# A two-layer transformer block on one core: context gates moved ahead of the keys' squares, level items computed in strips of 32, low-rank operands loaded and split first

## The chip, the core and the metric

The kernel runs on one NeuronCore of a Trainium2 chip. The metric is the time of one execution on the device, in microseconds. An execution of the kernel before took 905.5 us as the median of three runs (902.12 to 905.83). A fourth execution was profiled and took 903.21 us; its trace spans 901.3 us.

Engines are named as in the profile: PE is TensorE's matmul, PEld its weight load, DVE is VectorE, ACT is ScalarE, POOL is GpSimd, SP is SyncE.

## What is computed

A hybrid layer (attention beside gated linear attention, GLA) and a second layer (mLSTM and a gated embedding), both with a squared-ReLU MLP, over 256 tokens of width 1024 with a context of 256 tokens. The change touches GLA alone. What it computes, cut from the reference:

```python
def gla_log_decay(lowrank, w_gk, b_gk):
    g = jax.nn.log_sigmoid((lowrank @ w_gk + b_gk).astype(jnp.float32)) / GLA_GATE_NORM
    return gla_heads(g, GLA_DK)
...
    def step(state, inp):
        qc, kc, vc, gc = inp
        b = jnp.cumsum(gc, axis=2)
        o_inter = jnp.einsum('bhid,bhde->bhie', qc * jnp.exp(b), state)
        diff = jnp.where(mask, b[:, :, :, None, :] - b[:, :, None, :, :], -jnp.inf)
        a = jnp.einsum('bhid,bhjd,bhijd->bhij', qc, kc, jnp.exp(diff))
        o = o_inter + jnp.einsum('bhij,bhje->bhie', a, vc)
...
def gla_final_state(k, v, g):
    b = jnp.cumsum(g, axis=2)
    return jnp.einsum('bhtd,bhte->bhde', k * jnp.exp(b[:, :, -1:] - b), v)
```

It runs forward and backward in time, for 4 heads of 128 key dimensions, over the 256 tokens, with the context's final state (`gla_final_state`) as the first state.

## The kernel before

**Products.** Every large matrix product is computed in three terms: each operand is split into a rounded high part (ScalarE, `hi_part`, L1323) and the rest (VectorE, `lo_part`, L1788), and TensorE adds hi x hi, lo x hi and hi x lo (`product`, L751). Weights come from one stream of 512 KB units through a ring of four buffers (`raw`); SP issues a unit when the unit four places back has been split. A tile of weights is four units. `w_hi` and `w_lo` hold two tiles, so that a tile is split while the one before it is used; ScalarE may begin a tile when TensorE is through with the tile two places back.

**Order.** The order of all work is one list of steps, `PLAN1` for the first mixer. Each engine walks the list and does its share of each step, and semaphores tie the shares together. `woven` writes the steps of one tile: 8 or 16 pieces of six matmuls with the splits (`round`, `cut`) of the next tile and a list of side steps spread evenly between them. The tiles in question, in order, are gk and gq, lr (the low-rank product), kv, gv0, gv1, aq0, aq1, ga0, and later wbg0.

**The low-rank operands.** POOL loads nine small tensors (L710 to L715), all of which count up one semaphore. At the step `prepare` ScalarE waits for all nine and rounds `gate_w`, the signs and then `lr_w` and `mg_w`; VectorE subtracts. TensorE's `lr` group (L811, L813) waits for the low part of `lr_w`.

**Level items.** The triangular scores of a head are built by levels: the diagonal, then one item per width 128, 64, 32, ..., 1, where the decay between a query and a key is taken in two factors around a boundary of that width. There are 9 items a head and 36 in all (`N_ITEMS`). Each walks through the engines in three steps of `gla_level(s)`: VectorE forms the arguments (L2169), ScalarE their exponentials (L1530, two instructions), VectorE multiplies with keys and queries (`gx_z`, L2176), TensorE multiplies two 128x128 blocks (L1021; the diagonal item L1014) into one of three banks, and VectorE puts the wanted entries into the score tile `gx_s` (L2149 diagonal, L2153 width 128, L2157 masked for all others; `lv_put` counts). A put always reads 128x256. `level_steps` lists the 39 values of s with the decays, gates and query products of each head between them, 57 steps; they are spread over kv, gv0, gv1 and aq0.

**The context's state.** In tile aq1 the steps `gstate` 0 to 5 run a chain over the heads: gate matmuls (L984), three ScalarE passes for log(1 + exp) (L1489 to L1491), VectorE's L2113, cumulative sums on TensorE (L972, L974), their exponential (L1504), VectorE's product with the keys (L2108), and the state (L960). The gate matmuls of head 0 wait for all puts. The steps just before, `rope k 0` and `rope k 1`, sum the squares of the attention keys on VectorE (L2012, L2013), and in the second of them ScalarE waits for the variance (L1836) to begin its inverse root.

**The turn.** `yturn` (L897) transposes a quarter of the merged branches; the first of four is a side step of wbg0.

## Time and profile before

| | before |
|---|---|
| median of three runs | 905.5 us (902.12 to 905.83) |
| profiled execution | 903.21 us, span 901.3 us |
| TensorE matmul busy | 876.1 us, 97% |
| VectorE busy | 627.0 us, 70% |
| ScalarE busy | 482.6 us, 54% |
| mean granted clock of TensorE | 0.996 |
| moved by DMA | 162.25 MB, mean 180 GB/s |

How to read it: an engine's busy time is the union of its instructions' times, and matmuls overlap by their pipeline, so a busy PE is not yet PE at its pace; the distance from one start to the next tells the pace. The profile is of one execution, so sums of its durations are compared with its own 903.21 us. The granted clock is 1.00 at 2.4 GHz and 0.50 at 1.2 GHz.

### The profile page before, as it was taken

To read this page: it belongs to the slowest core of one execution; us is meant where nothing else is said; L and a number is where in the kernel's file an instruction comes from. 1 tells how busy PE (TensorE), PEld (TensorE's weight loads), DVE (VectorE), ACT (ScalarE), POOL (GpSimd) and SP (SyncE) were. 2 spreads that over 40 slices of the span, in tenths; PEclk is the share of its full clock that TensorE was granted. 3 is DMA by queue.
4 is the path that set the end of the run, shared out by engine and by line. 5 is a ranking of instruction groups with operands and counts; after the bars stand their busy time and mean duration, and the time that the engine had idled before them with its cause. 6 is when DMAs were issued, how large, how long until landed. Compare 5 with 4: busy or idle time off the path is not lost.

```text
span 901.3 us, 14166 instructions
## 1 busy us (share of the span) xinstructions
PE 876.1 (97%) x5136; PEld 755.5 (84%) x5136; DVE 627.0 (70%) x997; ACT 482.6 (54%) x758; POOL 13.1 (1%) x26
## 2 busy tenths in 40 slices
PE   5999999899999999999999999999999999999996
PEld 3878888787788888889999998998888999999985
DVE  3579979779788988865555557767787855555575
ACT  4576555465666565565444444454655644444454
POOL 0110000000000000000000000000000000000001
PEclk9999999999999999999999999999999999999999
DMA  9954323226347777735555558254444765555531
GB/s 364 374 141 140 117 71 112 99 94 204 124 142 234 260 266 257 242 126 189 187 187 186 186 186 280 94 187 138 145 138 142 248 223 205 180 190 191 183 119 48
DMA packets 45296, 162.25 MB, mean 180 GB/s; under 512 B 5500, under 2 KB 5644, under 8 KB 45248
## 3 DMA queue, kind: packets, MB, share of 16 engines
q1 hardware_dynamic: 43200, 156.78, 51.6%
q0 software_dynamic: 1328, 4.16, 1.6%
q8 instruction: 32, 0.52, 0.3%
q10 hardware_dynamic: 720, 0.65, 0.2%
q14 instruction: 16, 0.13, 0.0%
HBM read 160.52 MB, written 1.05 MB: 179 GB/s over the span
## 4 chain that ended last, share of the span: by engine, by line
PE 77%; DVE 11%; ACT 4%; DMA 3%; issue 3%; POOL 1%; POOLq 0%; DVEq 0%; SPq 0%; ACTq 0%
PE bank L751 65%; DVE w_lo L1788 3%; PE bank L939 1%; PE bank L1021 1%; ACT w_hi L1323 1%; DMA raw<-in_stream 1%; DMA arena<-in_early 1%; DVE small L1818 1%; PE bank L929 1%; PE bank L1221 1%; DMA gate_row<-in_b_gates 1%; PE bank L1041 1%; PE bank L1036 1%; DVE act_lo L1788 1%; PE bank L946 1%
## 5 line engine op out<-in xcount | busy, mean ns | idle before, releaser
L1788 DVE TENSOR_TENSOR w_lo<-raw,w_hi 128x1024 fp32r<-128x1024 f32 x244 | 288.3, 1220 | 150.7 <-ACT w_hi L1323 150.0
L1323 ACT ACTIVATE w_hi<-raw 128x1024 fp32r<-128x1024 f32 x244 | 245.8, 1050 | 193.2 <-PE bank L751 163.0
L751 PE MATMUL bank<-w_hi,act_lo 128*128 128x512 f32 (+1 forms) x728 | 293.2, 403 | 0.3 <-DVE w_lo L1788 0.2
L751 PE MATMUL bank<-w_lo,act_hi 128*128 128x512 f32 (+1 forms) x728 | 282.8, 388 | 0.0
L751 PE MATMUL bank<-w_hi,act_hi 128*128 128x512 f32 (+1 forms) x728 | 282.2, 388 | 0.0
L751 PE MATMUL bank<-act_lo,w_hi 128*128 128x256 f32 x640 | 182.9, 286 | 1.4 <-DVE act_lo L1788 0.9
L751 PE MATMUL bank<-act_hi,w_hi 128*128 128x256 f32 x640 | 181.0, 283 | 0.0
L751 PE MATMUL bank<-act_hi,w_lo 128*128 128x256 f32 x640 | 181.0, 283 | 0.0
L751 PEld LDWEIGHTS bank<-w_lo,act_hi 128*128 128x128 f32 x728 | 136.7, 188 | 29.3
L751 PEld LDWEIGHTS bank<-w_hi,act_lo 128*128 128x128 f32 x728 | 137.2, 188 | 27.4 <-issue 1.4
L751 PEld LDWEIGHTS bank<-w_hi,act_hi 128*128 128x128 f32 x728 | 137.3, 189 | 25.4 <-issue 1.0
L751 PEld LDWEIGHTS bank<-act_lo,w_hi 128*128 128x128 f32 x640 | 122.6, 192 | 4.9 <-DVE act_lo L1788 2.8
L751 PEld LDWEIGHTS bank<-act_hi,w_hi 128*128 128x128 f32 x640 | 122.7, 192 | 0.5
L751 PEld LDWEIGHTS bank<-act_hi,w_lo 128*128 128x128 f32 x640 | 122.7, 192 | 0.0
L1788 DVE TENSOR_TENSOR act_lo<-arena,act_hi 128x512 fp32r<-128x512 f32 x64 | 41.7, 686 | 5.3 <-ACT act_hi L1323 4.6
L1818 DVE SCALAR_TENSOR_TENSOR small<-raw,silu_c,small 128x512 f32<-128x512 f32 x56 | 42.0, 750 | 4.9 <-DMA raw<-in_stream 3.0
L1530 ACT ACTIVATE arena<-arena 128x256 f32<-128x256 f32 x64 | 24.1, 426 | 24.1 <-DVE arena L2169 23.9
L1323 ACT ACTIVATE act_hi<-arena 128x512 fp32r<-128x512 f32 (+1 forms) x33 | 20.0, 630 | 31.3 <-DVE arena L1915 25.5
L1394 ACT ACTIVATE arena<-bank 128x512 f32<-128x512 f32 x42 | 24.7, 590 | 14.2 <-PE bank L751 14.0
L2176 DVE TENSOR_TENSOR arena<-arena 128x512 f32<-128x512 f32 x32 | 21.9, 685 | 4.9 <-ACT arena L1530 4.8
L1021 PEld LDWEIGHTS bank<-arena 128*128 128x128 f32 x128 | 18.8, 190 | 5.1 <-issue 1.9
L939 PEld LDWEIGHTS bank<-arena 128*128 128x128 f32 x128 | 16.7, 191 | 7.2 <-issue 5.7
(264 smaller groups left out, 753.7 us busy)
## 6 DMA issues: line engine op xcount, KB each, us to landing
raw<-in_stream SPq DMA_DIRECT2D x278, 512.0 KB, 4.4
arena<-in_early SPq DMA_DIRECT2D x16, 512.0 KB, 10.7
res<-in_x SPq DMA_DIRECT2D x2, 512.0 KB, 4.2
arena<-in_ctx SPq DMA_DIRECT2D x2, 512.0 KB, 11.3
res<-in_x POOLq DMA_DIRECT2D x1, 1024.0 KB, 10.6
arena<-in_norm_final POOLq DMA_DIRECT2D x1, 512.0 KB, 4.3
arena<-in_ple_b POOLq DMA_DIRECT2D x1, 512.0 KB, 5.2
out<-arena ACTq DMA_DIRECT2D x2, 256.0 KB, 2.7
```

The lines of the kernel that those rows point to most:

```text
L751: last = pe.matmul(o, left, right, start=start and m == 0, stop=stop and m == 2, skip_group_check=shared)
L929: pe.matmul(psum[4 + i % 2][:, :], q_t[:, h, t * P:(t + 1) * P], k_t[:, h // (QH // KVH), :], start=True, stop=True).then_inc(score_done, 1)
L939: last = pe.matmul(psum[7][:, t * P:(t + 1) * P], kv[:, c, c0:c0 + HD], prob_t[:, c, :], start=(c == 0), stop=(c == 3))
L946: last = pe.transpose(psum[6][:, c * P:(c + 1) * P], prob[:, j % 3, c * P:(c + 1) * P], ident)
L1021: last = pe.matmul(o[:, t * P:t * P + P], z[:, 0, tile[t]], z[:, 1, queries], start=True, stop=True)
L1036: pe.matmul(o, gx_s[h][:, SCORE_BLOCK[j, t], :], gv[:, j, h * DV:(h + 1) * DV], start=(j == 0), stop=False)
L1323: return act.activation(o, i, ACT.Copy)
L1394: act.activation(o, i, ACT.Copy, scale=scale).then_inc(evac_act, 1)
L1530: ins = act.activation(gx_z[k % 3][:, m].rearrange("p (n h t) -> p n h t", h=2, t=LEVELS[k % N_LVL]), crossed(gx_d[k % 2], m, LEVELS[k % N ...
L1788: return dve.tensor_tensor(o, x, hi.bitcast(F32), ALU.subtract)
L1818: ins = dve.scalar_tensor_tensor(out=ada_sum, in0=w, scalar=c, in1=ada_sum, op0=ALU.mult, op1=ALU.add)
L2176: dve.tensor_tensor(gx_z[k % 3], gx_z[k % 3], keys_queries(h), ALU.mult).then_inc(lv_z, 1)
```

## The change

Four things are changed.

1. The gate matmuls, the three ScalarE passes of context head 0 leave `gstate` 0 and become a step `gsfirst` in tile aq0, ahead of `rope k 0`. VectorE's share stays in `gstate` 0.
2. Level items other than width 128 are computed by strips. A 128-token block is cut into four groups of 32 keys; each is its own matmul with 32 output partitions, and only with the 32 queries that it needs (64 at width 64). The diagonal and the widths 16 to 1 are gathered in a small tile `gx_c` of 128x2x32 by VectorE, with masks and puts of 32 columns. The items of width 128, 64 and 32 (`COPIED`) are copied into `gx_s` by ScalarE, without masks, in one, two and four instructions. A new step `expand` lets ScalarE copy `gx_c` into the diagonal blocks of `gx_s`, four instructions a head; `gla_out` waits for it (`gx_full`), and VectorE's diagonal item of head h waits for that of head h - 2. The list of level steps has 61 entries.
3. POOL issues the loads of `small`, `wgk` and `signs` first, on their own semaphore. `prepare` moves up by one piece and waits for these three alone, ScalarE rounds `lr_w` and `mg_w` ahead of `gate_w` and the signs, and VectorE converts a mask of 160 columns instead of 896. The side steps after `prepare` are shifted.
4. `yturn 0` comes behind the eighth piece of wbg0 instead of the seventh.

The core of the diff:

```diff
+COPIED = (1, 2, 3)
+PUT_AT, _n = {}, {True: 0, False: 0}
+for _i in range(N_ITEMS):
+    _k = _i % PER_HEAD in COPIED
+    _n[_k] += 1
+    PUT_AT[_i] = (_k, _n[_k])
...
             out.append(("queries", h - 1))
+            out.append(("expand", h - 1))
...
-    sides = [[], [("prepare",)], cut("kv", 0), [("evac", "gk", 2)] + cut("kv", 1), [("evac", "lr", 0), ("lrcut",)],
-             cut("kv", 2), cut("kv", 3), [("gate", 0)], [("evac", "gk", 3), ("log_decay", 0)]]
+    sides = [[("prepare",)], cut("kv", 0), cut("kv", 1), [("evac", "gk", 2)],
+             [("evac", "lr", 0), ("round", "kv", 2), ("lrcut",), ("cut", "kv", 2)], cut("kv", 3), [], [("gate", 0)],
+             [("evac", "gk", 3), ("log_decay", 0)]]
...
-    p.woven("aq0", lv[c:] + [k[0], k[1]])
+    p.woven("aq0", lv[c:] + [("gsfirst",), k[0], k[1]])
...
-    p.woven("wbg0", [None] * 6 + [y[0]] + [None])
+    p.woven("wbg0", [None] * 7 + [y[0]])
...
+            for target, name in ((small[:, 0:384], "small"), (wgk, "wgk"), (signs, "signs")):
+                pool.dma_start(target, a[name]).then_inc(small_in, 16)
             pool.dma_start(consts[:, 1:6], a["consts"][:, 1:6]).then_inc(params_in, 16)
-            for target, name in ((small[:, 0:384], "small"), (wgk, "wgk"), (rope[:, :, :, :], "rope"),
-                                 (mask_in, "lvl_mask"), (signs, "signs")):
+            for target, name in ((rope[:, :, :, :], "rope"), (mask_in, "lvl_mask")):
...
-            pool.dma_start(p_in, a["p_t"]).then_inc(p_loaded, 16)
+            pool.dma_start(p_in, a["p_t"]).then_inc(small_in, 16)
...
-                if h < GH:
-                    if h == 0:
-                        pe.wait_ge(lv_put, N_ITEMS)
-                        pe.wait_ge(gx_g, GH)
-                    else:
-                        pe.wait_ge(gs_g, h)
...
+                if 0 < h < GH:
+                    pe.wait_ge(gs_g, h)
+                    gla_context_gate(h)
+
...
+                if h == 0:
+                    pe.wait_ge(lv_put, PUT_AT[N_ITEMS - 1][1])
+                    pe.wait_ge(lv_copied, len(COPIED) * GH)
+                    pe.wait_ge(gx_g, GH)
...
                 if n >= 3:
-                    pe.wait_ge(lv_put, n - 2)
+                    wait_put(pe, n - 3)
                 o = level_bank(n)
                 tile = [slice(0, P), slice(P, T)]
                 if e == 0:
-                    for t in range(2):
-                        last = pe.matmul(o[:, tile[t]], gk_x[:, h, tile[t]], gq_x[:, h, tile[t]], start=True, stop=True)
+                    keys, queries = gk_x[:, h], gq_x[:, h]
                 else:
                     k = h * N_LVL + e - 1
                     pe.wait_ge(lv_z, k + 1)
-                    z = gx_z[k % 3]
+                    keys, queries = gx_z[k % 3][:, 0], gx_z[k % 3][:, 1]
+                if e == 1:
                     for t in range(2):
-                        queries = tile[1 - t] if e == 1 else tile[t]
-                        last = pe.matmul(o[:, t * P:t * P + P], z[:, 0, tile[t]], z[:, 1, queries],
-                                         start=True, stop=True)
+                        last = pe.matmul(o[:, tile[t]], keys[:, tile[t]], queries[:, tile[1 - t]], start=True, stop=True)
+                else:
+                    n_cols = 64 if e == 2 else 32
+                    for t in range(2):
+                        for p in range(4):
+                            first = t * P + (64 * (1 - p // 2) if e == 2 else 32 * (p ^ 1) if e == 3 else 32 * p)
+                            last = pe.matmul(o[32 * p:32 * p + 32, t * n_cols:(t + 1) * n_cols],
+                                             keys[:, t * P + 32 * p:t * P + 32 * p + 32], queries[:, first:first + n_cols],
+                                             start=True, stop=True, skip_group_check=True)
...
+                pe.wait_ge(gx_full, h + 1)
...
-                if h < GH:
-                    act.wait_ge(gs_mm, h + 1)
-                    log1p_exp(gs_a.rearrange("p t d n -> p (t d n)"), psum[4][:, :], gs_ln, h)
+                if 0 < h < GH:
+                    gla_context_gate(h)
...
+            def gla_copy(n):
+
+                h, e = n // PER_HEAD, n % PER_HEAD
+                act.wait_ge(lv_mm, n + 1)
+                bank, to = level_bank(n), gx_s[h]
+                blocks = lambda rows_, w: bank[rows_, 0:2 * w].rearrange("p (b i) -> p b i", b=2)
+                if e == 1:
+                    ins = act.activation(to[:, 2:4, :], blocks(slice(0, P), P), ACT.Copy)
+                elif e == 2:
+                    for a_, b_ in ((0, 64), (64, 0)):
+                        rows_ = slice(a_, a_ + 64)
+                        ins = act.activation(to[rows_, 0:2, b_:b_ + 64], blocks(rows_, 64), ACT.Copy)
+                else:
+                    for p in range(4):
+                        rows_, c0 = slice(32 * p, 32 * p + 32), 32 * (p ^ 1)
+                        ins = act.activation(to[rows_, 0:2, c0:c0 + 32], blocks(rows_, 32), ACT.Copy)
+                ins.then_inc(lv_copied, 1)
+
             def gla_level(s):
+                n = s - 3
+                if 0 <= n < N_ITEMS and PUT_AT[n][0]:
+                    gla_copy(n)
...
+            def gla_expand(h):
+
+                wait_put(act, (h + 1) * PER_HEAD - 1)
+                for p in range(4):
+                    rows_ = slice(32 * p, 32 * p + 32)
+                    ins = act.activation(gx_s[h][rows_, 0:2, rows_], gx_c[rows_, h % 2], ACT.Copy)
+                ins.then_inc(gx_full, 1)
...
-                    act.wait_ge(params_in, 16 * N_PARAMS)
+                    act.wait_ge(small_in, 16 * N_SMALL)
+                    hi_part(lr_w[:, :, 0:32], small[:, 0:256].rearrange("p (k n) -> p k n", k=KC)).then_inc(small_hi_done, 1)
+                    hi_part(mg_w[:, :, 0:16], small[:, 256:384].rearrange("p (k n) -> p k n", k=KC)).then_inc(small_hi_done, 1)
                     hi_part(gate_w, wgk).then_inc(small_hi_done, 1)
                     hi_part(gate_x[6 * RANK:GATE_K], signs).then_inc(small_hi_done, 1)
-                    hi_part(lr_w[:, :, 0:32], small[:, 0:256].rearrange("p (k n) -> p k n", k=KC)).then_inc(small_hi_done, 1)
-                    hi_part(mg_w[:, :, 0:16], small[:, 256:384].rearrange("p (k n) -> p k n", k=KC)).then_inc(small_hi_done, 1)
...
-                if 0 <= n < N_ITEMS:
+                if 0 <= n < N_ITEMS and not PUT_AT[n][0]:
...
-                    to = gx_s[h]
...
-                        dve.scalar_tensor_tensor(out=to[:, 0:2, :], in0=blocks, scalar=2.0,
-                                                 in1=ident.unsqueeze(1).broadcast_to([P, 2, P]), op0=ALU.mult,
-                                                 op1=ALU.mult).then_inc(lv_put, 1)
-                    elif e == 1:
-                        dve.tensor_copy(to[:, 2:4, :], blocks).then_inc(lv_put, 1)
+                        if h >= 2:
+                            dve.wait_ge(gx_full, h - 1)
+                        ins = dve.scalar_tensor_tensor(out=c, in0=blocks(whole, 32), scalar=2.0,
+                                                       in1=diag_block[:, :].unsqueeze(1).broadcast_to([P, 2, 32]), op0=ALU.mult,
+                                                       op1=ALU.mult)
                     else:
-                        dve.wait_ge(lv_put, n)
-                        mask = lvl_mask[:, e - 2, :].unsqueeze(1).broadcast_to([P, 2, P])
-                        dve.copy_predicated(to[:, 0:2, :], mask, blocks).then_inc(lv_put, 1)
+                        dve.wait_ge(lv_put, PUT_AT[n][1] - 1)
+                        mask = lvl_mask[:, e - 4, :].unsqueeze(1).broadcast_to([P, 2, 32])
+                        ins = dve.copy_predicated(c, mask, blocks(whole, 32))
+                    ins.then_inc(lv_put, 1)
...
+                    dve.wait_ge(small_hi_done, SMALL_HI["gate_w"])
...
                     dve.wait_ge(params_in, 16 * N_PARAMS)
+                    dve.tensor_reduce(diag_block[:, :], ident.rearrange("p (b i) -> p i b", b=4), AX, ALU.add)
                     dve.tensor_copy(lvl_mask[:, :, :], mask_in).then_inc(masks_ready, 1)
...
-    masks = np.zeros((P, N_LVL - 1, P), np.float32)
-    for n, s in enumerate(LEVELS[1:]):
-        same = i // (2 * s) == j // (2 * s)
-        masks[:, n] = same & ((i % (2 * s) < s) != (j % (2 * s) < s))
+    row, col = np.arange(P)[:, None] % 32, np.arange(32)[None, :]
+    masks = np.zeros((P, N_LVL - 3, 32), np.float32)
+    for n, w in enumerate(LEVELS[3:]):
+        same = row // (2 * w) == col // (2 * w)
+        masks[:, n] = same & ((row % (2 * w) < w) != (col % (2 * w) < w))
```

## Rows read from the trace of the kernel before

**Rows 1.** The page, part 1: busy us (share of the span) xinstructions.

```profile
PE 876.1 (97%) x5136; PEld 755.5 (84%) x5136; DVE 627.0 (70%) x997; ACT 482.6 (54%) x758; POOL 13.1 (1%) x26
```

**Rows 2.** Stretches: us, busy us (count) by engine, PE clock, DMA share, GB/s.

```profile
70.00:158.00 88.00, 86.60 (x452) 72.64 (x451) 80.15 (x137) 50.95 (x104) 0.00 (x0) 1.00 0.33 107
...
124.00:143.00 19.00, 18.20 (x93) 14.66 (x91) 17.09 (x29) 10.62 (x22) 0.00 (x0) 1.00 0.37 113
...
171.30:174.70 3.40, 3.40 (x15) 3.40 (x16) 3.14 (x10) 0.60 (x2) 0.00 (x0) 0.50 0.00 0
```

**Rows 3.** Timeline, 168 us: start, us, engine, line, form, count [idle before <-releaser].

```profile
167.79 0.39 PE L751 MATMUL bank<-w_lo,act_hi 128*128 128x512 f32 x1
...
171.27 0.80 PE L972 MATMUL bank<-arena,consts 128*128 128x128 f32 x2 [3.09 <-DVE arena L2113]
...
166.80 0.21 ACT L1424 ACTIVATE stat<-stat 128x8 f32<-128x8 f32 x1 [7.74 <-DVE stat L1836]
...
166.59 0.17 DVE L1836 TENSOR_SCALAR stat<-stat 128x8 f32<-128x8 f32 x1
...
170.52 0.69 DVE L2113 SCALAR_TENSOR_TENSOR arena<-bank,arena 128x512 f32<-128x512 f32 x1 [3.75 <-ACT arena L1491]
```

**Rows 4.** Timeline at 176 us, VectorE and TensorE.

```profile
175.31 0.69 DVE L2108 TENSOR_TENSOR arena<-arena 128x512 f32<-128x512 f32 x1
...
177.31 1.89 PE L960 MATMUL bank<-arena 128*128 128x256 f32 x8
```

**Rows 5.** TensorE's waits, 50 to 235 us: total us, times, longest.

```profile
PE bank L1021 <- DVE arena L2176: 1.4, 3, 0.6
```

**Rows 6.** Timeline at 56 us, TensorE and ScalarE.

```profile
56.05 0.39 PE L751 MATMUL bank<-w_lo,act_hi 128*128 128x512 f32 x1
57.15 0.42 PE L811 MATMUL bank<-act_hi,small_hi 128*64 128x512 f32 x1 [0.71 <-DVE small_lo L1788]
...
53.99 1.71 ACT L1323 ACTIVATE gate_r<-arena 98x1024 fp32r<-98x1024 f32 x2 [0.96 <-DMA gate_row<-in_b_gates]
```

**Rows 7.** Timeline at 77 us, VectorE.

```profile
77.26 0.41 DVE L2153 COPY res<-bank 128x256 f32<-128x256 f32 x1
77.59 0.68 DVE L2169 TENSOR_TENSOR arena<-arena 128x512 f32<-128x512 f32 x1
```

**Rows 8.** Timeline at 126 us, VectorE's z and TensorE's item.

```profile
125.75 0.69 DVE L2176 TENSOR_TENSOR arena<-arena 128x512 f32<-128x512 f32 x1 [4.59 <-ACT arena L1530]
...
126.60 0.67 PE L1021 MATMUL bank<-arena 128*128 128x128 f32 x4
```

**Rows 9.** Groups by form, ScalarE: count | busy us, mean ns | idle.

```profile
L1346 ACT ACTIVATE arena<-arena 128x256 f32<-128x256 f32 x2 | 0.8, 408 | 0.5 <-DVE arena L1982 0.5
...
L1425 ACT ACTIVATE stat<-stat 128x2 f32<-128x2 f32 x9 | 1.8, 204 | 0.3
```

**Rows 10.** Timeline at 79 us, TensorE around one level item.

```profile
78.66 0.39 PE L751 MATMUL bank<-w_lo,act_hi 128*128 128x512 f32 x1
...
79.57 0.40 PE L751 MATMUL bank<-w_hi,act_hi 128*128 128x512 f32 x1
```

**Rows 11.** Timeline at 18 us, TensorE around one modulation strip (L1243).

```profile
17.86 0.28 PE L751 MATMUL bank<-act_hi,w_lo 128*128 128x256 f32 x1
18.07 0.64 PE L1243 MATMUL bank<-arena,small 128*32 128x256 f32 x8
...
18.86 0.28 PE L751 MATMUL bank<-act_hi,w_hi 128*128 128x256 f32 x1
```

**Rows 12.** Chain of work that ended last: start, us, line, count.

```profile
278.67 0.86 PE bank L1041 x4
```

**Rows 13.** Timeline at 57 us, weight loads of TensorE.

```profile
57.12 0.13 PEld L811 LDWEIGHTS bank<-act_hi,small_hi 128*64 128x64 f32 x1 [1.11 <-issue]
57.18 0.11 PEld L813 LDWEIGHTS bank<-act_lo,small_hi 128*32 128x32 f32 x1
```

**Rows 14.** Table of stretches, as in rows 2.

```profile
230.00:390.00 160.00, 159.97 (x790) 131.57 (x789) 130.83 (x214) 96.16 (x154) 4.02 (x8) 1.00 0.65 215
```

More of the change, by code:

```diff
@@ L380 @@
 UP0 = {"a": 0, "b": 2 * FF_STEPS}
-N_FIRST, N_PARAMS = 2, 9
+N_FIRST, N_SMALL, N_PARAMS = 2, 3, 6
 GATE_K = 6 * RANK + 2
-SMALL_HI = {"lr": 4, "gate_x": 6, "p": 7}
+SMALL_HI = {"lr": 2, "gate_w": 4, "gate_x": 6, "p": 7}
 SMALL_LO = {"lr": 2, "gate_w": 3, "gate_x": 4, "p": 5}
@@ L621, in wait_block, with wait_put @@
             eng.wait_ge(turn_y_act if e else turn_y_dve, count)
+        def wait_put(eng, n):
+            copied, count = PUT_AT[n]
+            eng.wait_ge(lv_copied if copied else lv_put, count)
         def gain_shift(name):
@@ L976, in gla_state, with gla_context_gate @@
                 h = j
-                if h < GH:
-                    if h == 0:
-                        pe.wait_ge(lv_put, N_ITEMS)
-                        pe.wait_ge(gx_g, GH)
-                    else:
-                        pe.wait_ge(gs_g, h)
-                    for t in range(2):
-                        last = pe.matmul(psum[4][:, t * T:(t + 1) * T].rearrange("p (d n) -> p d n", d=2),
-                                         gate_x[:, T + t * P:T + (t + 1) * P],
-                                         gate_w.rearrange("p (d n) -> p d n", d=2)[:, :, h * P:(h + 1) * P],
-                                         start=True, stop=True)
-                    last.then_inc(gs_mm, 1)
+                if 0 < h < GH:
+                    pe.wait_ge(gs_g, h)
+                    gla_context_gate(h)
+            def gla_context_gate(h):
+                if h == 0:
[3 more added lines that the diff above has]
+                for t in range(2):
+                    last = pe.matmul(psum[4][:, t * T:(t + 1) * T].rearrange("p (d n) -> p d n", d=2),
+                                     gate_x[:, T + t * P:T + (t + 1) * P],
+                                     gate_w.rearrange("p (d n) -> p d n", d=2)[:, :, h * P:(h + 1) * P],
+                                     start=True, stop=True)
+                last.then_inc(gs_mm, 1)
             def gla_gate(h):
@@ L1012, in gla_level @@
                 if e == 0:
-                    for t in range(2):
-                        last = pe.matmul(o[:, tile[t]], gk_x[:, h, tile[t]], gq_x[:, h, tile[t]], start=True, stop=True)
+                    keys, queries = gk_x[:, h], gq_x[:, h]
                 else:
@@ L1017, in gla_level @@
                     pe.wait_ge(lv_z, k + 1)
-                    z = gx_z[k % 3]
+                    keys, queries = gx_z[k % 3][:, 0], gx_z[k % 3][:, 1]
+                if e == 1:
                     for t in range(2):
-                        queries = tile[1 - t] if e == 1 else tile[t]
-                        last = pe.matmul(o[:, t * P:t * P + P], z[:, 0, tile[t]], z[:, 1, queries],
-                                         start=True, stop=True)
+                        last = pe.matmul(o[:, tile[t]], keys[:, tile[t]], queries[:, tile[1 - t]], start=True, stop=True)
+                else:
+                    n_cols = 64 if e == 2 else 32
+                    for t in range(2):
+                        for p in range(4):
[3 more added lines that the diff above has]
+                                             start=True, stop=True, skip_group_check=True)
                 last.then_inc(lv_mm, 1)
@@ L1752, in _ @@
                     gla_keep(step[1])
+                elif kind == "expand":
+                    gla_expand(step[1])
                 elif kind == "merge":
@@ L2140, in gla_level @@
                 n = s - 3
-                if 0 <= n < N_ITEMS:
+                if 0 <= n < N_ITEMS and not PUT_AT[n][0]:
                     h, e = n // PER_HEAD, n % PER_HEAD
-                    to = gx_s[h]
                     dve.wait_ge(lv_mm, n + 1)
-                    blocks = level_bank(n).rearrange("p (b i) -> p b i", b=2)
+                    bank, c = level_bank(n), gx_c[:, h % 2]
+                    blocks = lambda rows_, w: bank[rows_, 0:2 * w].rearrange("p (b i) -> p b i", b=2)
+                    whole = slice(0, P)
                     if n == 0:
```

21 lines of the change are left out of this document (16 added, 5 removed).

## The prediction

> **What bounds the kernel now.** The page comes first: TensorE's matmuls fill 97% of the span [rows 1]. So time can only fall where TensorE waits, where its clock is low, or where its own work shrinks. The changed steps lie between 50 and 180 us. The table of stretches tells who is near the limit there [rows 2]: from 70 to 158 us PE is busy 86.6 of 88 us and VectorE 80.2, and from 124 to 143 VectorE has 17.1 of 19. I then took TensorE from start to start in the timeline, since the busy times of overlapping matmuls hide short gaps. A 512-column product starts every 0.23 us, a 256-column one every 0.12 [rows 10, 11].
>
> The one large wait is at 168 us [rows 3]. The last product starts at 167.79, so the next could start at 168.02, and the first cumulative sum of the context state (L972) starts at 171.27: 3.25 us. It waits for L2113 on VectorE (170.52), and that for three ScalarE passes. ScalarE had stood 7.74 us until 166.80 for the variance of the keys (L1836 at 166.59), with the gates queued behind. After the idle time comes a stretch of 3.4 us at granted clock 0.50, so at 1.2 GHz, which then returns to 2.4 [rows 2]. That costs half of 3.4, 1.7 us.
>
> **The change part by part.**
>
> *First context gates ahead of the keys' squares.* The two gate matmuls and ScalarE's three passes run before ScalarE blocks. VectorE's L2113 then follows L1836 at 166.8 and ends at 167.5, before TensorE asks at 168.02. Gain 3.25 + 1.7 = 4.95 us. TensorE meets no new wait at the new place: it comes two pieces of aq0 after the last level item, when the last puts are done. What is late next is L2108, the product of decays and keys, which ended 1.3 us ahead of L960 [rows 4]. In the new order VectorE does the k-norm, one w_lo and L2108 from 167.5 on (171.1 to 176.0 in the old order, 4.9 us), so it ends near 172.4, and L960 is wanted at 172.4 (177.31 less 4.95). I leave 0.2 us for it; bounds 0 and 2.
>
> *Low-rank operands landed and split first.* TensorE could start the low-rank product at 56.28 and starts at 57.15: 0.87 us, of which the profile calls 0.71 idle [rows 6]. ScalarE waited 0.96 us until 53.99 for the last of nine loads and split gate_w before the operand in question. New: three loads are issued first on POOL's queue, six behind them; ScalarE starts at 53.0 and the operand's halves are ready before 55. Gain 0.87. The constants, rope and masks now land behind three small loads; they are wanted at about 58, when the old order had them all by 53.99: cost nothing. The chain to the first level item (log decays, scans, first z) moves up by 1 us on ScalarE and more on VectorE, which converts a smaller mask; TensorE moves up by 0.87. L1021's first wait is at this item [rows 5].
>
> *Level items by strips: VectorE.* A put costs 0.33 us (77.26 to 77.59) [rows 7]. There are 28 masked ones, 4 diagonal and 4 copies: 36 x 0.33 = 11.9 us. After: 24 puts of 64 elements. No row has that form; the ends are 0.17 us (128x8, L1836) [rows 3] and 0.33. I take 0.17, the nearer in elements: 4 us. VectorE gains 8 us in 88. That is not on the path except where it bounds: L1021's three waits, 1.4 us idle together, the longest 0.6 [rows 5], and from start to start 0.16 more each, as at L811, so 1.9. All three go, unless something takes their place.
>
> *ScalarE's copies.* Per head one of 256 elements, two of 128, four of 64 and four for the expansion, between 0.20 (128x2) and 0.41 us (128x256) [rows 9]: 0.41 + 0.5 + 0.9 + 0.9 = 2.7 us, 11 in all. ScalarE has 51 of 88 us busy [rows 2], so it fits. Behind a copy waits the exponential of the next item, and behind that VectorE's z. The copy is for an item three steps back, which TensorE has finished. The expansion waits for the last put of its head, with the next head's exponentials queued behind it. I price both at 0.3 us; ends 0 and 3.
>
> *Level items by strips: TensorE.* An item now holds the stream for 0.45 us: product at 78.66, due again at 78.89, back in step at 79.34 (79.57 less 0.23) [rows 10]. 32 of the 36 items become eight matmuls of 32 output partitions and 32 columns (64 for one level): 16 weight loads and 16 matmul records instead of 4 and 4. The nearest row is the modulation strip, four matmuls into four partition groups of one bank [rows 11]. Its slot is 18.74 less 17.98, 0.76 us for 8 records of 256 columns. Such a record alone takes 0.215 us [rows 12], so 8 would take 1.72: the four groups run side by side, 0.43 us, and 0.33 us are lost in going to the narrow shape and back. With 32 columns four rounds stream 4 x 0.027, so 0.33 + 0.11 to 0.15 = 0.44 to 0.48. I take 0.46: 32 x 0.01 = 0.3 us. What the columns save, the change of shape takes. Ends: 0.43 (-0.6 us) and the whole 0.76 (+10).
>
> The strip's 0.33 us is the row for a rule that speaks against this part: "Mode switching requires drain" (the Trainium skill, TensorEngine Tiling (Array Packing), Tiling Modes); the trace agrees. With the fourfold speed that this page gives for 32 columns and no drain, an item would take 0.11 us, and 32 of them would save some 10 us.
>
> *What the narrow items do to issue.* In the strip all 8 records start within 0.26 us (0.64 less one of 0.38) [rows 11]. Where TensorE comes from a wait, the second weight load starts 0.06 us behind the first, though the weights are small [rows 13]. I take that for the pace at which pairs reach the engine. 16 pairs then need up to 0.96 us behind a late z, against 0.24 for four. Where z comes a microsecond early this hides under the product before (six products, 1.39 us). Just after a tile's start it doesn't: ScalarE's first rounding waits for the tile before, so z ends at 126.44 and the item starts at 126.60 [rows 8]. Three such places (in kv, gv1, aq0) at 0.6: 1.8 us. The plan also has 61 level steps for 57, so that two items come behind one product at four places (levels 10 and 11, 15 and 16, 31 and 32, 34 and 35), where the second isn't issued ahead: I take 0.33 each (0.96 less the first item's 0.46 and the 0.17 by which it may run on), 1.3 us; ends 0 and 2.
>
> *A turn one piece later.* y_turn (L897) in wbg0 moves from the seventh to the eighth piece, 1.39 us later. It isn't among TensorE's waits now: 0.
>
> From 180 us on nothing changes, TensorE has no gap to 390 and the transfers have room (0.65) [rows 14]: what is gained arrives.
>
> Sum: -4.95 - 0.87 - 1.9 = -7.7; +0.2 + 0.3 + 0.3 + 1.8 + 1.3 = +3.9. Net -3.8 us. The profiled execution took 903.2 us (span 901.3 and 1.9 around it), which gives 899.4. It lies 2.3 under the median of 905.5; the mean of all four is 904.2, which gives 900.4. I say 900.0.
>
> **The rivals.**
> - *Slower: issue doesn't keep up.* Every narrow item costs the strip's slot, 0.76, because its 16 pairs are never all at the engine when their turn comes: the items add 32 x 0.31 = 10 us, not 0.3: 910. It decides from 0.57 us an item on: (0.57 - 0.45) x 32 = 3.8. For it: loads 0.06 us apart after a wait. Against: 1.39 us is time for 23 pairs. Chance 0.15. A page has the rule for it: "With hardware decode off, the NX ucode spends ≈62 ns per MATMUL" (the Trainium skill, TensorE: Matmul & The Clock Gate, Part 1). Paid in full that would be 0.99 us an item and a time of some 920, by the page's figure.
> - *The wait moves.* The gates are early, but L2108 or ScalarE's copies are late, and TensorE waits 1.5 to 3 us before L960 or at items: 902 to 903. Chance 0.2.
> - *Strips pay.* The change of shape costs less at 32 columns and issue is hidden: items at 0.2 to 0.35 give 3 to 8 us, issue gives back 3: 889 to 895. Chance 0.1.
> - *The gates don't help*, since ScalarE blocks all the same: 4.95 us stay, 905. Chance 0.05; the order of steps is plain.
>
> **How the numbers follow.** Forecast case 0.5: 900.0, own range 897 to 902.5 by the bounds above. The range 892 to 909 leaves out two thirds of the first rival and a third of the third, 0.13, and the odd case. The runs shown scatter by 0.4%, so 0.5% (4.5 us from 905.5, below 901.0 and above 910.0) is about what can be told from no change. Faster: 0.1 + 0.36 of the forecast case + 0.02 = 0.48. Slower: 0.08 of the first rival, 0.02 for what I haven't thought of: 0.1. Within: 0.42.
>
> **What would show it.** Right: L972 starts in step with the product before it and the clock is 1.00 from 160 to 190; no gap before L811; puts on VectorE under 0.2; an item's slot 0.44 to 0.5, with 0.6 more after a tile's start. Wrong: narrow items at 0.6 or more each; a gap before L960; ScalarE's exponentials behind its copies; a low clock elsewhere.

## The result, and the profile after

| | before | after |
|---|---|---|
| median of five runs | 904.35 us | 896.34 us |
| profiled execution | 903.21 us | 895.88 us |
| VectorE busy | 627.0 us | 619.0 us |
| ScalarE busy | 482.6 us | 492.4 us |

The changed kernel takes 0.9924 of the time before (95% interval 0.9910 to 0.9938): 6.9 us less by that ratio, 8.0 by the medians, 7.3 between the two profiled executions. The forecast had the direction, and the time lies in its range of 892 to 909, but 0.7 us outside the 897 to 902.5 of its main case; the gain is about twice the 3.8 us of its sum. The ratios below leave out one execution, of gates_alone, that took 2254.6 us.

In the changed kernel L1042 is the item of width 128, L1048 every narrow item, L2246 the product z, L2226 the masked put, L1006 the context gates, L1904 the variance of the keys, L2181 what was L2113, L990 the first cumulative sum, L2176 what was L2108, L978 the state, L829 the low-rank product. The page's first part, then the table of stretches with the columns of [rows 2], the last two around the new place of L990:

```profile
PE 873.3 (98%) x5520; PEld 745.7 (83%) x5520; DVE 619.0 (69%) x986; ACT 492.4 (55%) x802; POOL 13.1 (1%) x26
```

```profile
70.00:158.00 88.00, 86.95 (x842) 64.45 (x841) 72.62 (x128) 61.38 (x147) 0.00 (x0) 1.00 0.32 105
124.00:143.00 19.00, 19.00 (x170) 14.18 (x170) 18.45 (x32) 11.72 (x29) 0.00 (x0) 1.00 0.45 146
165.00:168.00 3.00, 3.00 (x22) 2.75 (x21) 2.73 (x11) 2.52 (x4) 0.00 (x0) 1.00 0.02 5
168.00:172.00 4.00, 4.00 (x20) 3.38 (x19) 3.61 (x7) 3.44 (x6) 0.00 (x0) 1.00 0.41 126
```

From 70 to 158 us VectorE has 7.5 us less to do than in [rows 2] and ScalarE 10.4 more. The clock stays at 1.00 (2.4 GHz) where it was 0.50.

*The gates.* The timeline of the changed kernel from 160 us:

```profile
160.40 0.40 PE L1006 MATMUL bank<-gate_r 98*128 98x256 f32 x2
...
162.13 0.63 ACT L1522 ACTIVATE arena<-arena 128x512 f32<-128x512 f32 x1
...
164.14 0.17 DVE L1904 TENSOR_SCALAR stat<-stat 128x8 f32<-128x8 f32 x1
164.22 0.68 DVE L2181 SCALAR_TENSOR_TENSOR arena<-bank,arena 128x512 f32<-128x512 f32 x1
164.35 0.21 ACT L1455 ACTIVATE stat<-stat 128x8 f32<-128x8 f32 x1 [1.58 <-DVE stat L1904]
...
165.88 0.40 PE L769 MATMUL bank<-w_lo,act_hi 128*128 128x512 f32 x1
166.11 0.38 PE L990 MATMUL bank<-arena,consts 128*128 128x128 f32 x2
...
169.09 0.68 DVE L2176 TENSOR_TENSOR arena<-arena 128x512 f32<-128x512 f32 x1
...
170.44 1.89 PE L978 MATMUL bank<-arena 128*128 128x256 f32 x8
```

The passes end at 162.8, before the variance; L2181 follows it at once, and L990 starts 0.23 us behind the product before it, in step. L2176, feared late, ends 0.7 us ahead of L978. Compare [rows 3, 4].

*The low-rank product and the waits.* The timeline of 56 us and the waits of TensorE from 50 to 235 us (total us, times, longest):

```profile
53.33 0.41 ACT L1354 ACTIVATE small_hi<-small 128x256 fp32r<-128x256 f32 x1
...
53.97 0.42 DVE L1856 TENSOR_TENSOR small_hi<-small,small_hi 128x256 fp32r<-128x256 f32 x1 [0.22 <-ACT small_lo L1354]
...
56.45 0.39 PE L769 MATMUL bank<-w_lo,act_hi 128*128 128x512 f32 x1
...
56.67 0.39 PE L829 MATMUL bank<-act_hi,small_hi 128*64 128x512 f32 x1
```

```profile
PE bank L1048 <- DVE gx_c L2226: 1.0, 1, 1.0
PE bank L957 <- DVE act_lo L1856: 0.4, 1, 0.4
```

The gap of [rows 6] is gone, and so are the three item waits of [rows 5]; there is one new wait at an item, of 1.0 us. (The other one, 0.4 us, is in the kernel before too.)

*The narrow items.* The timeline around one item of 32 columns, around one of 64, and where two items stand together:

```profile
82.35 0.39 PE L769 MATMUL bank<-w_lo,act_hi 128*128 128x512 f32 x1
82.67 0.33 PE L1048 MATMUL bank<-arena 128*32 128x32 f32 x16
82.93 0.50 PE L769 MATMUL bank<-w_hi,act_lo 128*128 128x512 f32 x1
83.26 0.39 PE L769 MATMUL bank<-w_hi,act_hi 128*128 128x512 f32 x1
```

```profile
75.31 0.39 PE L769 MATMUL bank<-w_lo,act_hi 128*128 128x512 f32 x1
75.63 0.43 PE L1048 MATMUL bank<-arena 128*32 128x64 f32 x16
...
76.33 0.40 PE L769 MATMUL bank<-w_hi,act_hi 128*128 128x512 f32 x1
```

```profile
106.13 0.39 PE L769 MATMUL bank<-w_lo,act_hi 128*128 128x512 f32 x1
106.45 0.46 PE L1048 MATMUL bank<-arena 128*32 128x32 f32 x32
...
107.18 0.39 PE L769 MATMUL bank<-w_hi,act_hi 128*128 128x512 f32 x1
```

From product start to the second product start behind, less two paces of 0.23 (0.227 unrounded): 82.35 to 83.26 gives 0.46 us an item, the forecast's number. 64 columns: 0.57. Two items: 106.13 to 107.18 gives 0.59, so the second costs 0.13. Below, this distance less two paces is called an item's slot.

**Where TensorE stood.** All traces have the same 4104 products. The distance between the start of one and the same product in two traces says what was gained or lost up to there. The table takes the changed kernel as zero and sets all traces level at its 55 us, just ahead of lr; positive is later, in us. Between 60 and 155 us a row can be off by one item, 0.5 us, where the plans put items at other products; from 156 on all have the same work behind them:

```
at us of changed kernel      76     120     141     156     174     880
before                     +1.80   +1.87   +3.08   +2.31   +7.28   +7.65
u_gates                    -0.01   -0.06   -0.06   -0.05   +4.25   +4.31
u_lr                       +1.62   +1.58   +1.58   +1.57   +1.58   +1.61
u_levels                   -0.12   -0.04   +1.17   +0.81   +0.84   +0.87
gates_alone                +2.13   +2.20   +3.42   +3.04   +3.08   +3.14
double                     +0.26   +2.22   +3.33   +3.91   +3.91   +4.04
copies_dve                 -0.02   +0.16   +0.55   +1.19   +1.51   +1.63
exp_first                  -0.01   -0.01   +0.55   +0.22   +0.22   +0.27
expand_late                +0.01   +0.30   -0.14   +0.51   +0.50   +1.03
paired                     -0.58   -2.64   -2.84   -0.76   -0.77   -0.64
paired2                    -0.55   -2.66   -4.59   -1.73   -1.72   -1.26
paired3a                   -0.58   -2.40   -3.53   -3.90   -3.90   -3.82
paired3b                   -0.56   -2.67   -4.60   -4.56   -4.56   -4.19
```

The row of before is the bill: 1.80 us around lr and the first item of width 128, 0.5 in all that follows up to 156, 4.97 at the gates, 0.37 later.

### The profile page after: what moved, and what is told of

The parts are those of the page before. It is cut to its first block, busy times and chain, and to the rows that moved or that the text cites. A ratio compares the mean times of both kernels' runs of the same rounds, so it can differ in the third digit from the quotient of the medians.

```text
span 894.1 us, 14961 instructions
## 1 busy us (share of the span) xinstructions
PE 873.3 (98%) x5520; PEld 745.7 (83%) x5520; DVE 619.0 (69%) x986; ACT 492.4 (55%) x802; POOL 13.1 (1%) x26
## 4 chain that ended last, share of the span: by engine, by line
PE 87%; DVE 7%; ACT 3%; issue 2%; DMA 1%; SPq 0%; POOL 0%; POOLq 0%; DVEq 0%; ACTq 0%
PE bank L769 74%; DVE w_lo L1856 2%; PE bank L957 1%; PE bank L947 1%; PE bank L1250 1%; DMA arena<-in_early 1%; PE bank L1048 1%; PE bank L1070 1%; PE bank L1065 1%; ACT w_hi L1354 1%; PE bank L1272 1%; PE bank L905 1%; PE bank L964 1%; PE bank L978 1%; DVE act_lo L1856 1%
## 5 line engine op out<-in xcount | busy, mean ns | idle before, releaser
L2246 DVE TENSOR_TENSOR arena<-arena 128x512 f32<-128x512 f32 x32 | 22.0, 687 | 12.2 <-ACT arena L1586 12.1
L957 PEld LDWEIGHTS bank<-arena 128*128 128x128 f32 x128 | 16.7, 191 | 7.2 <-issue 5.7
L2295 DVE TENSOR_TENSOR arena<-arena 128x512 f32<-128x512 f32 x32 | 20.7, 685 | 2.4 <-ACT arena L1657 2.2
```

What stands on the lines that cost most here:

```text
L957: last = pe.matmul(psum[7][:, t * P:(t + 1) * P], kv[:, c, c0:c0 + HD], prob_t[:, c, :], start=(c == 0), stop=(c == 3))
L2246: dve.tensor_tensor(gx_z[k % 3], gx_z[k % 3], keys_queries(h), ALU.mult).then_inc(lv_z, 1)
L2295: dve.tensor_tensor(hid_h[:, g], hid_r[:, g], hid_r[:, g], ALU.mult).then_inc(hsq_done, 1)
```

## The experiments

Ratios are to the kernel before on the same chip, from five rounds (4 to 8 executions of each variant are counted), with 95% intervals; the changed kernel's is 0.9924 (0.9910 to 0.9938). Each kernel has one trace. For u_lr, u_levels, copies_dve, exp_first, expand_late, paired and paired2 the interval overlaps that of the changed kernel, so there the time alone proves no difference, and the argument rests on the place at which the trace shows it.

**u_gates.** The first context gates go back into `gstate` 0.

```diff
-    p.woven("aq0", lv[c:] + [("gsfirst",), k[0], k[1]])
+    p.woven("aq0", lv[c:] + [k[0], k[1]])
...
-                if 0 < h < GH:
-                    gla_context_gate(h)
+                if h < GH:
+                    gla_context_gate(h)
```

> The changed kernel with the first context gates back in gstate 0. Theory A (the three gains are separate and add): the wait before L990 and the low clock come back whole, +4.9 us against the changed kernel, about 901.2. Theory B (most of the gain is the freed VectorE: the variance comes earlier and the chain behind it is short anyway): +2 us or less, 898.3 or less.

Measured: 0.9968 (0.9956 to 0.9980), 4.0 us above the changed kernel; 4.3 in the trace, all between 156 and 174 us. The row of its waits:

```profile
PE bank L990 <- DVE arena L2182: 2.7, 1, 2.7
```

Theory A is the nearer one, but 4.3 us come back instead of 4.9. The wait is 2.7 instead of 3.1 us [rows 3], because the variance comes earlier, as theory B had it, though only by 0.4 us: it starts at 164.56, 1.63 us ahead of the last product before the wait; in the kernel before it starts at 166.59, 1.20 us ahead. From there to L2182 (L2113 before) it is 3.93 us in both.

**gates_alone.** The kernel before with this part only.

> The kernel before with the first context gates moved and nothing else. Theory A (this part alone brings what it brought in the sum, the 3.25 us wait and the 1.7 us of low clock): -4.9 us against the kernel before, ratio 0.9946. If VectorE's load of the old level items, which lies just ahead of it, left less room for the chain behind the gates, TensorE waits for it before L960: -3 to -4.

Measured: 0.9950 (0.9934 to 0.9965), 4.5 us less. Between 156 and 174 us its distance to the changed kernel grows by 0.04, that of before by 4.97: 4.93 us come from the move, with VectorE's old load in place. The forecast's 4.95 is shown for this stretch. Less arrives in the time, because 0.7 us are lost ahead of it: 0.3 at lr, where the last load lands later in this execution, and 0.4 at the last two level items. With one more step in aq0 these two stand behind one product, the second waits for z, and together they cost 1.30 us; in the kernel before they cost 0.45 each.

**u_lr.** Loads, ScalarE's rounding and the side steps in the old order (the smaller mask stays).

```diff
-    sides = [[("prepare",)], cut("kv", 0), cut("kv", 1), [("evac", "gk", 2)],
+    sides = [[], [("prepare",)], cut("kv", 0), [("evac", "gk", 2)] + cut("kv", 1), [("evac", "lr", 0), ("lrcut",)],
...
-            for target, name in ((small[:, 0:384], "small"), (wgk, "wgk"), (signs, "signs")):
-                pool.dma_start(target, a[name]).then_inc(small_in, 16)
             pool.dma_start(consts[:, 1:6], a["consts"][:, 1:6]).then_inc(params_in, 16)
+            for target, name in ((small[:, 0:384], "small"), (wgk, "wgk")):
+                pool.dma_start(target, a[name]).then_inc(small_in, 16)
```

> The changed kernel with the old order of the small loads, of ScalarE's rounding and of the side steps around lr. Theory A: the gap before the low-rank product comes back, +0.9 us, 897.2. Rival: the first level items, which come up to 1 us later, wait anyway, so the gap only moves: 0 to +0.3, 896.5.

Measured: 0.9939 (0.9925 to 0.9952), 1.4 us more; 1.6 in the trace, of which 0.7 just before lr, 0.2 at the gate matmuls behind it and 0.75 at the first item of width 128. Its waits:

```profile
PE bank L1042 <- DVE arena L2247: 0.5, 1, 0.5
PE bank L829 <- DVE small_lo L1857: 0.5, 1, 0.5
```

Both theories were too small. The first item's wait, one of the three of [rows 5], is not VectorE's puts (there are none yet): it comes with the late chain from `prepare` and the side steps to the first z.

**u_levels.** The level items of the kernel before, with the other parts in place.

```diff
-                else:
-                    n_cols = 64 if e == 2 else 32
-                    for t in range(2):
-                        for p in range(4):
...
+                    for t in range(2):
+                        queries = tile[1 - t] if e == 1 else tile[t]
+                        last = pe.matmul(o[:, t * P:t * P + P], z[:, 0, tile[t]], z[:, 1, queries],
+                                         start=True, stop=True)
```

> The changed kernel with the level items as before: 128x128 matmuls, all puts of 128x256 on VectorE, no ScalarE copies, 57 level steps. By the distances between product starts in the two traces the level items' part gave about 1.5 us net: 897.8. By the terms of the prediction (narrow items cost 0.3 + 1.8 + 1.3 + 0.3 more and save 1.9) undoing it would be 1.8 us faster: 894.5. If VectorE's load carries more than the three waits, 900 or more.

Measured: 0.9928 (0.9915 to 0.9942), which can't be told from the changed kernel; 0.87 us later in the trace. The largest part of the diff is worth 0.4 to 0.9 us; the prediction's terms, by which undoing it would be 1.8 us faster, don't hold. By its items: undone, items 25 and 28 wait again (1.04 and 1.18 us for 0.45; 1.4 us with the little one at 22); narrow items that stand alone get 0.01 us cheaper each, those of 64 columns 0.12 (0.8 in all); the two pairs cost 0.31 more each (0.6); and the last three cost 1.8 instead of 2.3. That is 1.4 - 0.8 + 0.6 - 0.5 = 0.7. In the kernel before the last three cost 1.35: the other 0.4 is the wait of gates_alone, which comes with the moved gates.

**double.** Every narrow item's matmuls issued twice in a row.

```diff
-                    for t in range(2):
+                    for t in (0, 1, 0, 1):
                         for p in range(4):
```

> The changed kernel with each narrow item's 16 matmuls issued twice in a row (the second 16 write the same results again). Theory C (what 16 more pairs cost is only their streaming, 0.13 us, 0.24 at width 64; the 0.33 is the change of shape): 28 x 0.13 + 4 x 0.24 = +4.6 us against the changed kernel, 901.0. Theory D, the prediction's (pairs reach the engine 0.06 us apart once the queue ahead is used up): the 16 more cost up to 0.96 each, +10 to +30 us.

Measured: 0.9968 (0.9957 to 0.9979), 4.0 us more; 4.0 in the trace. An item of 32 columns goes from 0.46 to 0.59 us, 8 ns for each more pair of weight load and matmul, and one of 64 from 0.57 to 0.79. That would be 4.5 us for all; at items 33 and 34 the added work falls into the wait. Theory D falls: pairs are not issued 0.06 us apart. They stream. What is left of an item without its 16 pairs is 0.33 us at 32 columns and 0.35 at 64, and two items doubled side by side cost 0.89, again 0.33 and four times 0.14. The items of four 128x128 matmuls have no such rest: four starts 0.11 us apart fill their slot of 0.45. So the rest is taken for the cost of the change of shape.

**copies_dve.** The copies of widths 128, 64 and 32 and the expansions go to VectorE.

```diff
-COPIED = (1, 2, 3)
+COPIED = ()
...
+                    if e == 1:
+                        ins = dve.tensor_copy(to[:, 2:4, :], blocks(whole, P))
...
+            def gla_expand(h):
```

> The changed kernel with the copies of widths 128, 64 and 32 and the expansions on VectorE, at the places of the plan at which ScalarE had them; ScalarE has no share in the items but its exponentials. Theory F (VectorE's relief removed the item waits; handing work back returns them): VectorE gets some 11 us back, and TensorE waits 1.5 to 2 us more for z: 898. Theory G (ScalarE's copies are what delays z at 152 us, 1.3 us of wait): that wait goes, 895, if VectorE's extra load costs nothing.

Measured: 0.9946 (0.9933 to 0.9959), 2.0 us more; 1.6 in the trace. Its stretch:

```profile
70.00:158.00 88.00, 86.37 (x837) 63.61 (x836) 80.90 (x165) 51.17 (x104) 0.00 (x0) 1.00 0.31 101
```

VectorE is back at the 80 us of [rows 2], and TensorE waits longer at four places (items 15, 28, 31 and 34), 0.1 to 0.5 us each. Of the kernel before's waits at items 25 and 28 only the second comes back, by 0.4 us. Theory F holds in size. Theory G falls: the wait at 152 us is there, and 0.5 longer.

**exp_first.** ScalarE's exponentials ahead of its copy in each level step.

```diff
             def gla_level(s):
-                n = s - 3
-                if 0 <= n < N_ITEMS and PUT_AT[n][0]:
-                    gla_copy(n)
...
                     ins.then_inc(lv_exp, 1)
+                n = s - 3
+                if 0 <= n < N_ITEMS and PUT_AT[n][0]:
+                    gla_copy(n)
```

> The changed kernel with ScalarE's exponentials of a level step ahead of its copy for the item three steps back. Theory G (the wait of 1.3 us at 152 us comes from the copy that stands ahead of the exponentials): z of that item is 0.9 us earlier, the wait falls to 0.4, 895.4. Theory H (the rounding of the weights ahead of both, 1.05 us, and the crowded plan make it late): 896.0 or more. A bank comes free up to 0.8 us later; if that matters anywhere, TensorE waits for ScalarE's copies and it is slower than the changed kernel.

Measured: 0.9931 (0.9917 to 0.9944), 0.6 us more; 0.3 in the trace. ScalarE and TensorE around the place, changed kernel first:

```profile
150.59 1.62 ACT L1586 ACTIVATE arena<-arena 128x256 f32<-128x256 f32 x4
...
151.40 0.69 DVE L2246 TENSOR_TENSOR arena<-arena 128x512 f32<-128x512 f32 x1 [1.72 <-ACT arena L1586]
152.01 0.22 DVE L2226 COPY_PREDICATED gx_c<-lvl_mask,bank 128x64 f32<-128x64 uint8 x1
...
152.24 0.33 PE L1048 MATMUL bank<-arena 128*32 128x32 f32 x16 [1.04 <-DVE gx_c L2226]
```

```profile
151.03 0.77 ACT L1583 ACTIVATE arena<-arena 128x256 f32<-128x256 f32 x2
151.70 0.88 ACT L1572 ACTIVATE res<-bank 32x64 f32<-32x64 f32 x4
...
152.63 0.51 PE L1048 MATMUL bank<-arena 128*32 128x32 f32 x32 [0.80 <-ACT res L1572]
```

The wait mostly changes its name. The view of the changed kernel names the put L2226, which is for another bank; z (L2246) ends at 152.1, 0.15 before the item starts. With the order turned, TensorE waits for the four copies (0.88 us), because they free the bank, and z of the second item ends only at 152.53, just before them. The two items then cost 1.51 us instead of 1.85, but item 24 now waits 0.55 us for copies where it didn't wait before. ScalarE has a rounding, four copies and four exponentials to do for two items that the plan put in one piece; neither order of copies and exponentials helps, and the rounding's place wasn't tried.

**expand_late.** The expansions of heads 2 and 3 move to ga0, so that the list is two steps shorter.

```diff
-            out.append(("expand", h - 1))
+            if h < 3:
+                out.append(("expand", h - 1))
...
-    p.woven("ga0", [gs[4], q[1], gs[5], None, q[2], ("qkturn", 0), q[3]])
+    p.woven("ga0", [gs[4], q[1], gs[5], [("expand", 2), ("expand", 3)], q[2], ("qkturn", 0), q[3]])
```

> The changed kernel with the expansions of heads 2 and 3 moved from the level steps to ga0, so that the list has 59 level steps and the last tile's steps lie further apart. Theory G: the 1.3 us wait of the item at 152 us goes, 895.0. Rival: ScalarE is still behind there, because its copies of width 32 and a rounding stand ahead of the exponentials: same time, 896.3.

Measured: 0.9937 (0.9924 to 0.9950), 1.2 us more; the wait stays (1.1 us), and ga0 loses 0.4. Theory G falls here too.

**paired.** A narrow item is held back until the next one, so that two share one stay in the narrow shape.

```diff
+        def paired(n):
+
+            return n % PER_HEAD in (2, 4, 6, 8) and n < N_ITEMS - 1
...
-                if not 0 <= n < N_ITEMS:
+                if not 0 <= n < N_ITEMS or paired(n):
                     return
...
+                for m in (n - 1, n) if n and paired(n - 1) else (n,):
+                    gla_item(m)
```

> The changed kernel with narrow items held back on TensorE until the next one, so that two stand in one stay in the narrow shape (widths 64 and 32, 16 and 8, 4 and 2, 1 and the next diagonal): 15 pairs, of which the plan had 2. Theory C (the 0.33 us is paid once for each stay in the narrow shape; a second item costs 0.13): -0.33 x 13 = -4.3 us, 892.0. Theory D, the prediction's (the second item's 16 pairs reach the engine 0.06 us apart and cost 0.79): each new pair gains 0.46 + 0.46 - 0.46 - 0.79, so it is slower by 4 us or the same. Rival E: exponentials and puts wait for the held-back items, because their buffers come free a step later, and TensorE then waits for z: -4.3 + 3 or more, 895 to 898.

Measured: 0.9906 (0.9893 to 0.9920), 1.6 us less, which the intervals don't tell from the changed kernel; 0.6 in the trace. Theory C holds up to 129 us, where ten pairs, at 0.59 to 0.69 us each, have brought TensorE 3.4 us. Then most of it is lost: 0.3 us at item 25, 0.9 at item 28, 1.0 at items 33 and 34 beyond what the changed kernel waits there, and the rest in a stretch of low clock behind them (152 to 155 us: granted 0.58).

**paired2.** With the expansions late as well.

> The paired kernel with the expansions of heads 2 and 3 in ga0. In the paired kernel TensorE had gained 4.0 us at 130 us of the trace and lost 3.4 of it up to 155 us, to four late z and to a stretch of low clock behind the last. Theory G (the crowded steps of the last head make z late): at least the wait at 150 us and the low clock go, 893 or less. Rival E (held-back items free their buffers too late whatever the plan): the waits stay, 895.6.

Measured: 0.9922 (0.9907 to 0.9937), the same as the changed kernel; 1.3 us ahead in the trace. The lead of some 4 us at 141 falls to 1.7 at 156. Up to item 28 VectorE is the bound (columns as above):

```profile
125.00:140.00 15.00, 13.62 (x149) 10.27 (x148) 14.16 (x26) 8.91 (x23) 0.00 (x0) 1.00 0.46 160
```

**paired3a and paired3b.** The pairs, exponentials first, items 29 and 30 apart, and two of ada6's four products, each 1.5 us of VectorE, moved to gv0, where VectorE had stood for 5.8 us; 3b with the late expansions too.

```diff
-    at = {1: 0, 3: 1}
+    at = {1: 0, 3: 1, 11: 2, 14: 3}
...
-    at = {7: 2, 9: 3}
-    p.woven("gv1", [[step, ("ada", 6, at[i])] if i in at else step for i, step in enumerate(lv[b:c])])
+    p.woven("gv1", lv[b:c])
```

> The paired kernel with the exponentials ahead of the copies, items 29 and 30 not paired, and two of the four side products of ada6 (1.5 us of VectorE each, at 133.6 and 136.9 us of the changed kernel's trace) moved into gv0, where VectorE stood idle for 5.8 us behind ScalarE's first rounding. Theory K (pairing gained its 0.33 a pair, and VectorE's and ScalarE's work behind 125 us then bounded): VectorE gets 3 us of room, the waits for z behind 130 us shrink to 1 us or less, and the kernel comes to 893. Rival E (buffers of held-back items): the waits stay, 895.6.

> paired3a with the expansions of heads 2 and 3 in ga0 too. Theory K: as paired3a, 893, and up to 0.6 us less by the shorter list of steps. Rival: late level steps in gv1 gain nothing, as in the kernel where the expansions alone were moved: the same as paired3a or 0.5 us more.

Measured: 0.9882 (0.9867 to 0.9897) and 0.9882 (0.9867 to 0.9898); medians 892.9 and 892.2. Both beat the kernel before by 10.7 and the changed one by 3.8 us, 3.8 and 4.2 in the trace. What TensorE has gained at 141 now arrives. A pair in 3b and its only wait at an item:

```profile
84.98 0.39 PE L773 MATMUL bank<-w_lo,act_hi 128*128 128x512 f32 x1
85.30 0.46 PE L1058 MATMUL bank<-arena 128*32 128x32 f32 x32
...
86.02 0.39 PE L773 MATMUL bank<-w_hi,act_hi 128*128 128x512 f32 x1
```

```profile
PE bank L1058 <- DVE gx_c L2236: 1.0, 1, 1.0
```

Theory K holds for the sum; which of the companions of the pairs did how much wasn't separated, and so it isn't shown that VectorE's moved work was the one that counted.

## Why the prediction was right, and where its size was off

- **Gates, -4.95:** right in place, mechanism and size (4.97 between the traces, 4.93 alone in this stretch, 4.3 in u_gates). L2108's 0.2 was 0: the product came 0.7 us early.
- **Low-rank, -0.87:** right for the gap (0.89 between the traces, 0.70 in u_lr); the whole part is worth 1.4 to 1.6. The first item's wait belongs here, and the forecast had booked it under VectorE's relief.
- **Item waits, -1.9:** all three went, 2.1 us by their slots. Of VectorE's part 1.4 is left, by u_levels. That VectorE's load was the cause is shown in part: copies_dve gives it back, and 0.4 us return at item 28, none at item 25. The forecast compared unlike numbers: 0.33 us is the distance from a put's start to the next start, 0.17 the length of a record. The masked put is now 0.22 us long (0.44 before) and the next instruction starts 0.13 behind it. By that VectorE gains more than the 8 us forecast, 11.9 less 24 x 0.13 = 8.8; the stretch shows 7.5, and the rest wasn't followed.
- **A narrow item, 0.46:** exact for 32 columns. The item of width 64 costs 0.57; the forecast counted it as the others, 4 x 0.11 = 0.4 us short.
- **Issue behind a late z, +1.8: the first term that failed; it cost nothing.** It took the 0.06 us between two weight loads in [rows 13] for the pace of pairs. After its wait, the item at 152.24 lets the next product start 0.26 us later, as at 82.67, where z had been 3 us early. The double kernel gives 8 ns a pair. That is also far from the 62 ns per MATMUL that the page named in the forecast gives for hardware decode off (the Trainium skill, TensorE: Matmul & The Clock Gate, Part 1), which doesn't bind here. (In the forecast's own terms 0.99 us an item would have made 917 us, not 920.) Nor was z late at 126: it ended 0.55 us ahead, and item 22 cost 0.47. The drain at a change of mode (the Trainium skill, TensorEngine Tiling (Array Packing), Tiling Modes) agrees with the traces: 0.33 us, once a stay in the narrow shape.
- **Double places, +1.3: failed in mechanism and size.** At two of them two narrow items stand together and cost 0.33 less than apart, since the 0.33 is paid once; with a wide item beside it (items 9 and 10) nothing changes. At the fourth, items 33 and 34, the pair doesn't form: the second waits for z, and the two cost 1.85 us, 0.9 more than two that stand apart. The net is +0.3.
- **ScalarE, +0.3:** its copies and expansions take 11.0 us, as forecast. No wait of TensorE follows from them but at items 33 and 34, where they stand ahead of the exponentials; how much of the 0.9 is theirs isn't shown.
- **The turn, 0:** about right. The distance between the two traces is 7.29 us ahead of the first turn, 7.39 behind it and 7.17 behind the second. No run tests this part alone.

By TensorE's slots the kernel before loses 0.9 us before lr, 0.3 at the gate matmuls behind it, 0.8 at the first item, 1.4 at items 22, 25 and 28, and 0.6 where the changed kernel has its two pairs. It saves 0.5 at the items of width 64, 0.3 at the other narrow ones and 0.95 at items 33 and 34. That is 2.2 us of the 2.31 at 156 us, and with the 4.97 at the gates 7.2 of the 7.28 at 174 us. Another 0.37 arise past 174 us and are in no term and no experiment. Undone one at a time, the three parts come to 4.3 + 1.6 + 0.9 = 6.8 us, since they aren't wholly separate.

So the gain was forecast at half its size mostly because of two terms: they weighed 3.1 us of costs that came to 0.3, which is 2.8 of the 3.5 us between the forecast's 3.8 and the 7.3 at 174 us. Smaller misses make up the rest, among them the 0.3 us at the gate matmuls behind lr, which no term held. That the time still lies in the range owes something to the range's width. Of the rivals, issue that doesn't keep up fell with the double kernel. "The wait moves" came true at one item, for 1.0 us, instead of 1.5 to 3. "Strips pay" came within 1.3 us of the time (889 to 895 for 896.3), but not by its reason: items cost 0.46, not 0.35.

## What to carry to other kernels

Price a change of the matmul's shape by stay, not by instruction: here 0.33 us in and out, for 16 to 64 pairs of weight load and matmul between, so gather narrow work. A long wait that starves TensorE can be paid twice, as idle time and as low clock, and moving a short chain ahead of a long one on the engine that both need can be the best part of a large diff. A gain on TensorE lasts only as far as the engines that feed it have room behind it: the pairs brought 3.4 us and kept 0.6, until VectorE's work was moved into a stretch in which it stood and ScalarE's exponentials came first.

## What was not expected of the hardware

- **Matmuls of 32 output partitions and 32 columns stream 8 ns apart**, each with its own weights (0.13 us for 16 more in an item), while the same engine starts a 512-column product every 227 ns.
- **The start of a launch varies.** In the traces of three kernels TensorE began with a stretch of low clock, ahead of anything that their edits touch; from 17 to 20 us u_levels and the changed kernel have:

```profile
17.00:20.00 3.00, 2.73 (x12) 2.63 (x12) 1.44 (x2) 1.06 (x1) 0.00 (x0) 0.55 1.03 412
```

```profile
17.00:20.00 3.00, 2.81 (x25) 2.27 (x26) 1.18 (x2) 1.06 (x1) 0.00 (x0) 1.00 1.04 414
```

  By the same product's start it is worth 1.5 us in each of the three (u_levels, double and paired3a), as much as several of the effects measured here, and a median of a few executions carries it: those of paired3a took 892.05, 892.08, 893.67 and 893.86 us. Aligning traces by the product takes it out.
